# Setup of a two-block layer stack in the order of need: x turned in parts, norm rows ahead of the Toeplitz write, bias read per layer

## What is computed

```
def first_block(x, p, ffn1_norm, ffn1_wi, ffn1_wo, mix_norm, w_in, ..., rel_bias, ...):
    for i in range(DEPTH):                                   # DEPTH = 2
        x = x + 0.5 * swiglu_ffn(rmsnorm(x, ffn1_norm[i]), ffn1_wi[i], ffn1_wo[i])
        z = rmsnorm(x, mix_norm[i]) @ w_in[i]
        hA = mlstm_chunkwise(...)
        hB = swa_sink_attention(..., sinks[i], rel_bias)     # window of 128, banded blocks
        x = x + (gated mix of hA and hB) @ w_out[i]
        x = x + 0.5 * swiglu_ffn(rmsnorm(x, ffn2_norm[i]), ffn2_wi[i], ffn2_wo[i])
        x = x + gate(x) * (p[i] @ w_ple[i])

def swa_sink_attention(q, k, v, q_gain, k_gain, sinks, rel_bias):
    dist = np.arange(Wn)[:, None] + Wn - np.arange(2 * Wn)[None, :]
    bias = rel_bias[t5_bucket(dist)]                         # one value per distance and head
    logits = where(valid, q k^T + bias, -inf)
```

## Time and profile before

| | |
|---|---|
| median of three runs | 3871.23 us (3866.43 to 3871.86) |
| span of the profiled execution | 3867.6 us; no other time of this execution is at hand |
| PE busy | 3661.1 us (95%) |
| PE weight loads busy | 2828.9 us (73%) |
| DVE busy | 1841.0 us (48%) |
| POOL busy | 1404.7 us (36%) |
| ACT busy | 1006.2 us (26%) |
| moved by DMA | 309.79 MB, mean 80 GB/s |

### The profile page before, as it was taken

How to read it: one execution, slowest core, us unless ns; L and a number is a source line. 1 busy time by engine, 2 the same in 40 slices (tenths; PEclk the granted TensorE clock), 3 DMA queues, 4 the chain that set the end, 5 groups by cost and what they waited for, 6 DMA issues and landing times.

```text
span 3867.6 us, 44550 instructions
## 1 busy us (share of the span) xinstructions
PE 3661.1 (95%) x15582; PEld 2828.9 (73%) x15582; DVE 1841.0 (48%) x2258; ACT 1006.2 (26%) x1320; POOL 1404.7 (36%) x581
## 2 busy tenths in 40 slices
PE   3999999999999999999999999898899999889997
PEld 2888865778887788875678888664688876467886
DVE  3542224754424542323665422757463554748163
ACT  1222223322222222222422222333221123322111
POOL 1444432334443444331234443321244432114442
PEclk6999999999999999999999999888999998899998
DMA  3332321223322332231223323211133231113231
GB/s 92 106 98 93 96 68 49 71 82 98 98 97 86 96 96 94 84 90 44 66 78 101 98 98 96 71 32 30 54 104 97 94 87 37 36 44 91 94 98 60
DMA packets 473852, 309.79 MB, mean 80 GB/s; under 512 B 16809, under 2 KB 432531, under 8 KB 473715
## 3 DMA queue, kind: packets, MB, share of 16 engines
q1 hardware_dynamic: 470224, 305.16, 26.4%
q10 hardware_dynamic: 3491, 2.80, 0.5%
HBM read 304.25 MB, written 3.67 MB: 80 GB/s over the span
## 4 chain that ended last, share of the span: by engine, by line
issue 65%; POOL 24%; PE 9%; POOLq 1%; DVE 0%; ACT 0%; DVEq 0%
POOL wl L421 24%; PE bank L444 2%; PE bank L443 2%; PE bank L439 2%; PE bank L462 1%; PE bank L458 1%; PE bank L464 1%; POOLq L420 0%; POOLq L418 0%; PE bank L465 0%; DVE y_sb L2014 0%; PE mb L503 0%; DVE var L1444 0%; DVE var L1424 0%; POOLq L421 0%
## 5 line engine op out<-in xcount | busy, mean ns | idle before, releaser
L421 POOL TENSOR_TENSOR wl<-raw,wh 128x1024 fp32r<-128x1024 f32 x576 | 1404.3, 2440 | 2413.1 <-ACT wh L1093 2412.8
L1093 ACT ACTIVATE wh<-raw 128x1024 fp32r<-128x1024 f32 x576 | 607.1, 1056 | 1626.0 <-PE bank L458 793.6
L458 PE MATMUL bank<-xh,wh 128*128 128x512 f32 x2528 | 995.9, 394 | 3.5 <-DVE xl L1418 3.5
L462 PE MATMUL bank<-xl,wh 128*128 128x512 f32 x2528 | 990.2, 392 | 0.0
L464 PE MATMUL bank<-xh,wl 128*128 128x512 f32 x2212 | 866.5, 392 | 0.0
L458 PEld LDWEIGHTS bank<-xh,wh 128*128 128x128 f32 x2528 | 478.4, 189 | 119.3 <-issue 18.5
L462 PEld LDWEIGHTS bank<-xl,wh 128*128 128x128 f32 x2528 | 478.7, 189 | 99.2
L444 PE MATMUL bank<-hh,wl 128*128 128x512 f32 (+1 forms) x1216 | 485.1, 399 | 0.0
L464 PEld LDWEIGHTS bank<-xh,wl 128*128 128x128 f32 x2212 | 418.8, 189 | 88.8
L443 PE MATMUL bank<-hl,wh 128*128 128x512 f32 (+1 forms) x1216 | 479.2, 394 | 0.0
L439 PE MATMUL bank<-hh,wh 128*128 128x512 f32 (+1 forms) x1216 | 476.8, 392 | 0.0
(11 more groups left out here) (358 smaller groups left out, 3439.5 us busy)
## 6 DMA issues: line engine op xcount, KB each, us to landing
raw<-in_ffn_wi_dram SPq DMA_DIRECT2D x176, 512.0 KB, 3.8
raw<-in_mlp_w_dram SPq DMA_DIRECT2D x128, 512.0 KB, 3.8
raw<-in_w_in_dram SPq DMA_DIRECT2D x102, 512.0 KB, 3.7
raw<-in_ffn_wo_dram SPq DMA_DIRECT2D x88, 512.0 KB, 3.6
raw<-in_w_out_dram SPq DMA_DIRECT2D x32, 512.0 KB, 3.9
raw<-in_w_ple_gate_dram SPq DMA_DIRECT2D x16, 512.0 KB, 3.6
raw<-in_w_a_dram SPq DMA_DIRECT2D x8, 512.0 KB, 3.5
raw<-in_w_b_dram SPq DMA_DIRECT2D x8, 512.0 KB, 3.4
```

The lines of the kernel that those rows point to most:

```text
L421: gp.tensor_tensor(wl[j][:], raw[j % RAW_SLOTS][:], wh[j][:].bitcast(F32), ALU.subtract)\
L458: first = pe.matmul(out[0:width, :], h[:, c:c + width], rh[:, k, :], start=k == 0, stop=False)
L462: pe.matmul(out[0:width, :], h[:, c:c + width], rl[:, k, :], start=False, stop=False)
L1093: act.activation(wh[n % SPLIT_SLOTS][:], raw[n % RAW_SLOTS][:], ACT.Copy).then_inc(s.hi_ready, 1)
```

## The change

SP loads the identity alone, then x in four parts of 128 tokens with a semaphore each, then the rest of the constants, then the nine small transfers that ACT issued, then `gate_raw` and the slabs. PE turns seven tiles of each part as it lands, into eight banks, with the bias matmul after the second part; the eighth tile's bank serves that matmul first, and its four turns come after DVE has read it. DVE copies four tiles, ACT four. PE waits for the norm rows alone before it turns them, and for constants and small transfers before the first slab. ACT issues the norm rows first and the Toeplitz write behind them. The row's buffer moves into the place of `bias`; so the waits at the head of each FFN go, and SP reads `bias` once per layer, after the last slab of the first FFN. What is multiplied in the layers is the same.

```
-            sp.dma_start(const[:], a["const_pack"]).then_inc(s.setup_const, 16)
-            sp.dma_start(x_tok[:], a["x"].rearrange("b (t p) d -> p (b t) d", p=P)).then_inc(s.setup_x, 16)
+            sp.dma_start(ident, a["const_pack"][:, C_IDENT:C_IDENT + P]).then_inc(s.setup_ident, 16)
+            for t in range(NT):
+                sp.dma_start(x_tok[:, t, :], a["x"][0, t * P:(t + 1) * P, :]).then_inc(x_landed[t], 16)
+            sp.dma_start(const[:, P:CONSTS], a["const_pack"][:, P:CONSTS]).then_inc(s.setup_const, 16)
...
+                sp.wait_ge(s.toep_out, 16)
+                need = sp.lower_val(tiles_out(Block1, L, T_FFN1 + 43))
+                sp.dma_start(bias[:], bass.AP(scratch.tensor, P - 1, [[TOEP - 1, P], [P * TOEP, SW_H], [1, 2 * P]]))\
+                  .wait_op(s.tile_evacuated, need, "sem-ge").then_inc(s.toep_in, 16)
...
+            pe.wait_ge(s.setup_ident, 16)
+            for t in range(NT):
+                pe.wait_ge(x_landed[t], 16)
+                for j in range(KT - 1):
+                    last = turn(x_banks[j][:, t * P:(t + 1) * P], x_tok[:, t, j * P:(j + 1) * P])
+                if t == 1:
+                    pe.wait_ge(s.setup_rel, 3 * 16)
+                    pe.matmul(B7[0:SW_H, 0:TOEP], rel[:], onehot[:], start=True, stop=True).then_inc(s.rel_psum, 1)
+            last.then_inc(s.setup_t, 1)
+            pe.wait_ge(s.toep_row, 1)
+            for t in range(NT):
+                last = turn(B7[:, t * P:(t + 1) * P], x_tok[:, t, (KT - 1) * P:KT * P])
+            last.then_inc(s.setup_t, 1)
+            pe.wait_ge(s.setup_rows, 16 * N_ROWS)
+            pe.wait_ge(s.setup_copied, 2)
...
+            pe.wait_ge(s.setup_const, 16)
+            pe.wait_ge(s.setup_small, 16 * N_SMALL)
+            pe.wait_ge(s.consts_ready, 1)
+            pe.wait_ge(s.setup_copied, 4)
+            pe.wait_ge(s.setup_copied_act, 4)
...
-            act.wait_ge(s.toep_row, 1)
-            act.dma_start(scratch, toep[:, None, :].to_broadcast([SW_H, P, TOEP]))\
-               .then_inc(s.toep_out, 16)
...
+            act.wait_ge(s.toep_row, 1)
+            act.dma_start(scratch, toep[:, None, :].to_broadcast([SW_H, P, TOEP])).then_inc(s.toep_out, 16)
+            act.wait_ge(s.setup_t, 1)
+            for j in range(4, KT):
+                if j == KT - 1:
+                    act.wait_ge(s.setup_t, 2)
+                act.activation(x_sb[:, j, :], (bank[j - 2][:] if j < 6 else (B6, B7)[j - 6]), ACT.Copy)\
+                   .then_inc(s.setup_copied_act, 1)
...
             def ffn(L, k, g, g_next, t, silu0):
                 norm(Block1, L, k, g)
-
-                dve.wait_ge(s.toep_out, 16)
-                dve.drain()
...
-                dve.wait_ge(s.toep_in, 16)
+                dve.wait_ge(s.toep_in, at(L, 16, 16))
```

More of the change, by code:

```diff
@@ L164, in program @@
         rope = place("rope", [MLA_D, 2, S], offset=bias_at)
+        toep = place("toep", [SW_H, TOEP], offset=bias_at)
         region = cursor[0]
@@ L180, in program @@
         rel = at_kb("rel", 23, [32, SW_H])
-        toep = at_kb("toep", 24, [SW_H, TOEP])
         proj = at_kb("proj", 0, [P, 18, S])
@@ L251, in program @@
         scratch = nc.dram_tensor("toeplitz_rows", [SW_H, P, TOEP], F32, kind="Internal").ap()
-        names = """split_done slab_used hi_ready tile_ready tile_evacuated setup_x setup_const setup_small setup_rel
+        names = """split_done slab_used hi_ready tile_ready tile_evacuated setup_const setup_ident setup_rows setup_small setup_rel setup_copied_act
             setup_t setup_copied rel_psum toep_row toep_out toep_in consts_ready
@@ L269, in program @@
         sm = {n: sem(n) for n in names}
+        x_landed = [sem(f"x_landed{t}") for t in range(NT)]
         raw_landed = [sem(f"raw_landed{n}") for n in range(RAW_SLOTS)]
@@ L310, in rows2c @@
                 return w[bass.ds(L, 1), sl, c0:c0 + S].rearrange("l (k p) c -> p (l k) c", p=P)
-            sp.dma_start(const[:], a["const_pack"]).then_inc(s.setup_const, 16)
-            sp.dma_start(x_tok[:], a["x"].rearrange("b (t p) d -> p (b t) d", p=P)).then_inc(s.setup_x, 16)
+            sp.dma_start(ident, a["const_pack"][:, C_IDENT:C_IDENT + P]).then_inc(s.setup_ident, 16)
+            for t in range(NT):
+                sp.dma_start(x_tok[:, t, :], a["x"][0, t * P:(t + 1) * P, :]).then_inc(x_landed[t], 16)
+            sp.dma_start(const[:, P:CONSTS], a["const_pack"][:, P:CONSTS]).then_inc(s.setup_const, 16)
+            with nc.allow_non_contiguous_dma("parameters of a few bytes"):
+                for dst, name in ((b_gate[:, :, 0:1], "b_igate"), (b_gate[:, :, 1:2], "b_fgate"),
+                                  (dt_bias[:, :, None], "ssd_dt_bias_2"), (dt_a[:, :, None], "ssd_a_log_2")):
+                    sp.dma_start(dst, a[name].rearrange("l (h o) -> h l o", o=1)).then_inc(s.setup_small, 16)
+                sp.dma_start(bs_rows[:], a["gmlp_b_s_2"].rearrange("l h t -> h l t")).then_inc(s.setup_small, 16)
+                sp.dma_start(sinks[:].rearrange("p l h -> p (l h)"),
+                             a["sinks"].rearrange("(o l) h -> o (l h)", o=1).to_broadcast([P, 2 * SW_H]))\
+                  .then_inc(s.setup_small, 16)
+                for half in range(2):
+                    src = a["ssd_d_2"].rearrange("l (i two) -> two l i", two=2)[half:half + 1]
+                    sp.dma_start(d_skip[half * 64:half * 64 + 64], src.to_broadcast([64, 2, 3])).then_inc(s.setup_small, 16)
+            sp.dma_start(sel4[:], a["sel4"]).then_inc(s.setup_small, 16)
             def ffn(L, wi, wo, n):
@@ L505, in turn @@
                 return pe.matmul(out, in_, const[0:k, C_IDENT:C_IDENT + k], start=True, stop=True)
[L508 to L523, removed]
+            x_banks = [B4, B5, bank[0][:], bank[1][:], bank[2][:], bank[3][:], B6, B7]
+            pe.wait_ge(s.setup_ident, 16)
[13 more added lines that the diff above has]
+            pe.wait_ge(s.setup_copied, 2)
             for l in range(2):
@@ L1248, in _ @@
                                      (rows2, Q_CB, 5, "ssd_conv_b_2")):
-                act.dma_start(dst[r0:r0 + n, :, :], a[name].rearrange("l (r c) -> r l c", c=P)).then_inc(s.setup_small, 16)
+                act.dma_start(dst[r0:r0 + n, :, :], a[name].rearrange("l (r c) -> r l c", c=P)).then_inc(s.setup_rows, 16)
             act.dma_start(rows1[R_MLOUT:R_MLOUT + ML_H, :, :], a["ml_out_norm"].rearrange("l h c -> h l c"))\
-               .then_inc(s.setup_small, 16)
+               .then_inc(s.setup_rows, 16)
             for r0, name in ((R_QN, "q_norm"), (R_KN, "k_norm")):
@@ L1254, in _ @@
                     act.dma_start(rows1[r0:r0 + 1, :, half * 64:half * 64 + 64], a[name].rearrange("(o l) c -> o l c", o=1))\
-                       .then_inc(s.setup_small, 16)
+                       .then_inc(s.setup_rows, 16)
             act.dma_start(rows2[Q_CW:Q_CW + 20, :, :], a["ssd_conv_w_2"].rearrange("l k (r c) -> (k r) l c", c=P))\
-               .then_inc(s.setup_small, 16)
-            act.dma_start(rows3[:], a["final_norm_g_2"].rearrange("(r c) -> r c", c=P)).then_inc(s.setup_small, 16)
@@ L1259, in _ @@
[L1259 to L1273, removed]
+               .then_inc(s.setup_rows, 16)
+            act.dma_start(rows3[:], a["final_norm_g_2"].rearrange("(r c) -> r c", c=P)).then_inc(s.setup_rows, 16)
+            act.wait_ge(s.toep_row, 1)
+            act.dma_start(scratch, toep[:, None, :].to_broadcast([SW_H, P, TOEP])).then_inc(s.toep_out, 16)
@@ L1483, in _ @@
             dve.tensor_tensor(toep[:], B7[0:SW_H, 0:TOEP], pad[:], ALU.add).then_inc(s.toep_row, 1)
[L1484 to L1487, removed]
+            dve.wait_ge(s.setup_t, 1)
+            for j in range(4):
+                dve.tensor_copy(x_sb[:, j, :], (B4, B5, bank[0][:], bank[1][:])[j]).then_inc(s.setup_copied, 1)
+            dve.wait_ge(s.setup_t, 3)
             dve.tensor_copy(p1[:], B4[:, 0:2 * R1])
@@ L1494, in _ @@
             dve.drain()
+            dve.wait_ge(s.setup_copied_act, 4)
             first_half(Block1, None, 0, g_first)
@@ L1733, in _ @@
                 norm(Block1, L, 1, par1[:, R_MIX:R_MIX + KT])
+                dve.wait_ge(s.setup_small, 16 * N_SMALL)
                 dve.tensor_copy(b_gate_now[:, None, :], b_gate[:, bass.ds(L, 1), :])
@@ L2024 @@
 ML_OFF = [0, 512, 896, 1152]
-N_SMALL = 11 + 1 + 4 + 2 + 4 + 2 + 2 + 1
+N_ROWS = 11 + 1 + 4 + 2
+N_SMALL = 4 + 1 + 1 + 2 + 1
 def constants(np):
```

## The result

| | before | after |
|---|---|---|
| median | 3869.7 us of 4 runs (3866.43 to 3871.86) | 3846.32 us of 4 runs (3844.78 to 3847.46) |
| ratio | | 0.9942, 95% interval 0.9928 to 0.9956 |
| span of the profiled execution | 3867.6 us | 3845.7 us |

The kernel is faster by 23.4 us, 0.6%.

What follows compares the result with a forecast made beforehand. The bound was a chain of transfers before the first matmul, with the Toeplitz write filling its queue; slab 0's high half beginning at 48, not 67.89, takes 20 us off the median 3871.23: 3851, range 3840 to 3860.

Steps and rivals of the forecast that it cites:

- what bounded the kernel: Head, before the first layer's first matmul at 72.17 us: a chain of transfers, not arithmetic; the write runs to 43.5.
- they land before 14: Norm rows, first on ScalarE's queue: 18 issues end at about 9.7 us, and the rows land before 14.
- slab 0 lands at about 48: Slab 0's load, queued on SP under the Toeplitz write: lands at about 48 us, with 45.5 and 52 as ends.
- 0.25 us a row and one piece per row: Engines holding the write: each row takes 0.25 us, one piece of SP's queue per row, so 16 us a slab.
- 19.9 us: The sum: high half of slab 0 begins at 48 us, not 67.89, and everything after is earlier by 20 us.
- the early slab: Rival at the head: slab 0 lands at 30 us, slab 1 at 46; 27 us gained, 3844; chance 0.20.
- The rival that came true: Slab 0 gets through early: TensorE does the first quarter, then stands until about 50 us; 3844, chance 0.20.
- The clock gives and takes nothing: First matmuls: TensorE comes out of idleness at a granted clock of 0.50, as before, so no time changes.
- The forecast of the write's end (45.0): Toeplitz write behind the norm rows: issued at about 10.3 us, not 8.81, so by its own length it ends at 45.0.
- the sign of being right: At the head: ScalarE idle after the squares until raw lands, at 46 to 52 us.
- the edits with no price: FFN-head waits dropped and bias read on SP's queue before slab 66: covered, though a read takes 12.0 us; no cost.
- The write does not hold the slabs: Rival at the head: slabs are not delayed by the Toeplitz write, the 47 us count in full; 3824, chance 0.08.

Runs made afterwards that it cites:

- The two-step write: The changed kernel with the Toeplitz row stored to HBM once, then copied there 128 times by a second transfer, 128 outermost: 3827.0 us, ratio 0.9895.

## Why the prediction was right, and where it was not

**Right: what bounded the kernel.** The chain back from the first matmul to the write, its half of the engines and 31 to 35 us, and that the change pays by starting earlier and by nothing else. The two-step write shows it from the other side: done in 6 us, the write holds no slab. The Trainium skill, "DMA: Bandwidth & Descriptors", section Rules for kernel authors, states that an outermost dimension of size c below 16 confines a DMA to at most c engines, and that a multiple of 16 belongs outermost. The trace agrees: share 0.47 with 8 outermost, 0.92 with 128. That the rows became nearly three times as quick as well is another matter, on which the prediction had nothing.

**Wrong: "they land before 14".** The rows were issued by 10.1 (forecast 9.7), but landed at 18.9, and ScalarE came to the high half of slab 0 at 25.76, not at 20.8. The step failed because it looked at ScalarE's queue alone. Without d_skip the rows are turned at 15.43, with d_skip as one row at 15.79: so some 3 us of the delay are the 4 B pieces on the other queue; the rest, 1 to 1.5 us, is not split up. The write's rows also flow only from about 16, not from 12: from 14 to 16 ScalarE's queue has 19 packets and moves next to nothing, from 16 to 17 it moves 0.03 MB.

**Wrong: "slab 0 lands at about 48".** It landed at 19.8. The term was the count of pieces ahead of it: d_skip and `gate_raw` were to go through one per row of the write, until 36 to 41. In fact the 4 B pieces kept the write's rows waiting as well, until about 16 (without d_skip ScalarE's queue moves 0.08 MB from 12 to 14, here nothing to speak of), and when these came they did not at once take turns with SP's queue piece by piece. Pieces under 512 B, gate_raw's among them, number 720 from 17 to 18 and 12 in the two microseconds after; then slab 0 came with 301 GB/s, beside the write's first rows:

```profile
q1 hardware_dynamic: 823, 0.42, 69.8%
q10 hardware_dynamic: 121, 0.19, 36.3%
```

These are the packets from 18 to 20 us of SP's queue (q1) and ScalarE's (q10), with their megabytes and share: nearly seven pieces to a row, or over three on the write's half of the engines if the pieces are spread evenly, and a row takes an engine 0.10 us on average (121 at 36.3% of 16 engines over 2 us). From 21 on it takes 0.24. So 0.25 us a row and one piece per row were right for the long stretch and wrong for the write's beginning; why its first rows are quicker, no run shows. So the sum's "19.9 us" was about the right size on the wrong slab: the early slab's gain of a quarter's 12 matmuls was not in it.

**The rival that came true, and its size.** "Slab 0 at 30, slab 1 at 46, TensorE stands until about 50": measured 19.8, 48.1 and 51.75. From 77.12 to 51.75 are 25.4 us. Of these 2.2 are given back: before, the second quarter followed on the first without a stand and ran from its first matmul at 0.23 us each, with the granted clock back at 2.4 GHz; now TensorE stood 16.31 us, and the first 9 matmuls take 4.0 us, 0.44 each, at 1.2 GHz:

```profile
54.90 0.63 PE L463 MATMUL bank<-xl,wh 128*128 128x512 f32 x1
55.32 0.57 PE L464 MATMUL bank<-xh,wl 128*128 128x512 f32 x1
55.73 0.39 PE L459 MATMUL bank<-xh,wh 128*128 128x512 f32 x1
55.96 0.39 PE L463 MATMUL bank<-xl,wh 128*128 128x512 f32 x1
```

Starts are 0.42 apart up to 55.73 and 0.23 from there on. "The clock gives and takes nothing" had reckoned with one start, not two. 23.2 us remain, the distance of the two sums of squares (85.34 and 62.14).

**Why forecast and result lie together all the same.** Both ends hang on the write's. The last wait that matters ends when the write does: with slab 0 as the prediction had it, with slab 1 in fact, at 48.13 us. The forecast of the write's end (45.0) was about 2 us early: 9 packets of ScalarE's queue still lie between 47 and 48, none after. So that the figure came out near was in part luck. By the prediction's own signs its path was wrong (a high half at 25.76, where 46 to 52 was the sign of being right), and the measured time lies nearer to the rival's 3844 than to 3851.

**Right: the edits with no price.** The bias read was issued at 385.65 and landed in 6.3 us, not 12.0. Slab 66's rounding, 421.57 in the earlier trace rows, is at 398.37, earlier by the same 23.2 us as the sum of squares, so nothing was lost between:

```profile
398.37 1.06 ACT L1119 ACTIVATE wh<-raw 128x1024 fp32r<-128x1024 f32 x1 [4.54 <-PE bank L459]
```

A second read per layer cost nothing either.

**The other rivals.** "The write does not hold the slabs" has its answer in 48.1. The Trainium skill's rule beside it ("DMA: Bandwidth & Descriptors", section Queues, rings and completion order: an engine drains a packet of typically 9 to 17 descriptors before it turns to the next queue) does not show here. The packets of the two queues are one to one in the kernel before from 20 to 32 us:

```profile
q10 hardware_dynamic: 376, 0.58, 45.7%
q1 hardware_dynamic: 378, 0.19, 5.3%
```

In the kernel after, from 21 to 31 and then from 33 to 40 us, they are:

```profile
q10 hardware_dynamic: 318, 0.49, 47.0%
q1 hardware_dynamic: 2, 0.00, 0.1%
...
q10 hardware_dynamic: 217, 0.33, 45.7%
q1 hardware_dynamic: 235, 0.12, 5.6%
```

Equal counts alone would also come out of turns of 9 rows and 9 pieces. But a row and a piece take an engine 0.26 us together, and in the kernel before each queue has 8 packets from 20.00 to 20.26 and 8 again from 20.26 to 20.52, one for each engine of the write: the turns are of one.

**What stays open.** From 21 to 31 slab 1 got nothing, and then its piece per row. What waited was, by the bytes, its half on the write's engines: by 21 SP's queue had moved 0.82 MB from 14 us on, which is slab 0 (0.52), gate_raw (0.03) and half of slab 1. It is so in three kernels: the changed one, the one with the write ahead, and the one with the second read. There slab 1's issue began within 1 us of the write's (11.6 and 10.82; 10.6 and 10.32; 11.1 and 10.89). In the kernel before and in the ones without d_skip and with x in one load it began 2 to 5 us ahead (6.8 and 8.81; 8.4 and 10.82; 10.9 and 15.69), and the stretch without a piece was 1 to 3 us, not 10 (14 to 15, 15 to 17 and 20 to 23). With two writes there was none: slab 0 itself was under the write there. That the slab's issue is worked off behind the write's would fit; no run was made that sets the two apart.

## What to carry to other kernels

Before transfers are put into another order, look at the share of DMA engines that a long one occupies: here 0.46 stood for a write of 1.5 MB that kept half of the engines for over 30 us, and storing the row once and copying it from HBM with 128 as outermost dimension gained as much as the reordering. Look at the time of a row too (0.24 against 0.08 us): the number of engines was only part of it. A transfer that holds engines is not harmless where it is moved to; ask which load will be under it there and who wants that load next. And count pieces, not bytes: 768 pieces of 4 B on one queue delayed the other queue's rows by some 3 us.

## What was not expected of the hardware

- One queue can hold the other with the DMA engines nearly idle: from 11 to 14 us these were busy 0.05 and moved 0 to 1 GB/s, while norm rows and write on ScalarE's queue and slab 0 on SP's had been issued. In those 3 us 310 packets of SP's queue were counted and 4 of ScalarE's; without d_skip the norm rows were turned 3.5 us earlier. What works that slowly no row names.
- The write's rows were not all alike: 0.10 us of an engine each from 18 to 20 us, 0.24 from 21 to 31, in the same transfer.
- The issue of a second write behind the first stopped ScalarE's queue for 12.07 us (11.53 to 23.60), as the norm row behind the write did before (12.86 us in the earlier trace rows).
